# Splitting a token list's output in two, and placing the next one-hots later

## The chip, the cores and the metric

The kernel runs on one core of one Trainium2 chip. The metric is the device time of one execution in microseconds (us), of which the kernel before took 897.17 us (median of 3 runs, 896.05 to 897.62).

## What is computed

One decoder layer for 256 prompt tokens and 8 sample tokens of width 1024: a token mixer of four branches, then a mixture of experts with 64 SwiGLU experts of inner width 256, eight chosen for each token, and one shared expert, then a final norm. The change lies in the mixture of experts; of the reference that is

```python
def moe_ffn(h, router_w, router_bias, e_gate, e_up, e_down, s_gate, s_up, s_down):
    ...
    gates = jnp.zeros((n, N_EXPERTS), jnp.float32).at[jnp.arange(n)[:, None], idx].set(w)
    hg = jnp.einsum('nd,edf->nef', h, e_gate)
    hu = jnp.einsum('nd,edf->nef', h, e_up)
    act = jax.nn.silu(hg) * hu * gates[:, :, None].astype(h.dtype)
    routed = jnp.einsum('nef,efd->nd', act, e_down)
    shared = (jax.nn.silu(h @ s_gate) * (h @ s_up)) @ s_down
    return routed + shared
```

## The kernel before

**Jobs and groups.** The mixer and the routing take the first 356 us or so. After them the 64 experts are worked off as 64 jobs in 16 groups of four (i is the group, j the job). The experts are sorted by how many tokens they have. A job has room for 128, 64 or 32 rows: in a full group (3 to 13) the four jobs have 128, 32, 64 and 32 rows, in the light groups at the start and the end 32 or 64. Groups 4 to 12 run in a hardware loop of the same code. The rows of a group lie in two sheets of up to 128 rows: in a full group sheet 0 holds job 0, and sheet 1 jobs 1 to 3.

**Lists.** Which tokens belong to a job of the next group is found out during this group, one list in each job. VectorE writes one-hots (`one_hot`, L2167 to L2177, three instructions at L2176 that compare slot numbers with a row order), TensorE multiplies them by a table (`token_list`, L1188, products at L1199), and VectorE takes from the result the row numbers into `idx` (L2192 or L2195) and the gates into `gcol` (L2193 or L2196). Both stand in `list_out` (L2179), and only the second one counts up the semaphore `lst_ready`. TensorE's next list waits for it, as the bank is used again, and so does GpSimd, which starts the gather of a sheet (`gather`, L807 to L816) when all its lists are there. The gates of the next group take the place of those of this group, so `list_out` waits with `act_ready` for the gating of the same job of this group (L2188).

**A job on the engines.** TensorE: up products (`up`, L1231, products at L1246 for 32 rows, L1249 for 128, L1251 and L1252 for 64), in their middle the turning of the activations of the job before (L891), then the list products; in job 1 the sums of the sheets done so far (`sums`, L1312, eight sums of 264 columns in three banks, products at L1334); where a sheet is due, the turning of its gathered rows (`turn_rows`, L1203, products at L891); last the down products of the job before (L1283 for 32 rows, L1292 for 128, L1298 and L1301 for 64). ScalarE: silu (L1673), copy of half of the turned rows (L1657), activations (L1665), outputs (L1687, L1690). VectorE: gating, that is silu times up times gate (`gated`, L2224, L2232), the other half of the turned rows (`rows_out`, L2210, L2213), the additions of the sums (`add_sums`, L2281, L2289), the spreading of token numbers (`sheet_to_tokens`, L2274, L2278) and the low parts of the outputs (`y_out`, L2235, L2247). GpSimd has nothing but the gathers (L814) in this stage, each behind its lists and behind the turning of the sheet that had the buffer before.

**Order by hand.** Each engine has its own `body(i)`, and the order of the calls in it is the order on the engine. VectorE's is the one that changes (L2324). In job 0 of a full group it is gating, list of the next group, one-hots for the next list, copy of rows of sheet 1; in job 1 the additions stand there, in job 2 the spreading, and in job 3 the copy of rows of the next group's sheet 0; the outputs of the job before come last. TensorE's up products of job 1 wait for both copies of sheet 1. The fourth of the eight sums waits for the first addition, as it has the same bank, and the eighth for the sixth (L1327 and L1328).

**Weights.** SyncE loads the weights of each job, 3 x 1 MB: gate and up when the up products of the job four before have ended, down when its down products have (`reload`, L670, issues at L652, L653 and L656). There are four slots.

Of the kernel before, what the change touches and what calls it, by code (L numbers as in the profile page):

```python
# [11 lines left out]
ALU = mybir.AluOpType  # L12
# [49 lines left out]
LIST_BANK = 7  # L62
# [59 lines left out]
BIG = 4096.0  # L122
# [3 lines left out]
UNROLL = 4  # L126
# [3 lines left out]
FIXED = 2  # L130
# [26 lines left out]
def bass_decoder_step(nc, x_prompt, x_sample, state_conv, state_pool, state_conf, c_prompt, c_sample,  # L157
# [6 lines left out]
    with ExitStack() as ctx:  # L164
# [137 lines left out]
        def in_mid(n):  # L302
# [52 lines left out]
        names = """cnt_ready ld_c ya_ready v_stored row_out rows_spread sh_load ld_mod2 consts tables_zero x2_sq  # L355
                   sh_down_load h2_stored up_done down_done x_xt x_w tokens_in to_token_ready bank3_copied bank4_gated sum_full sum_taken token_taken acc_gated rest_zero last_sum x_fin x_gated x_added
                   fin_ready out_done pool_chain ld_stage wg_masked states_done w_hi w_lo h2_ready
                   lst_ready xt_done dma_may_go ys_act ys_dve x2_ready
                   ld_fin x_idx x_gat x_y x_sc st_stored c_silu
                   x_norm h_split v_ready ws_ready ld_param pooled_ready g2_rows dconv_ready sq_ready  # L360
                   y_split m_split sel_ready h_raw oh_ready list_done act_ready
# [94 lines left out]
        def rows_used(i, j):  # L456

            if isinstance(i, int) and i == 0:
                return ROWS_OF_FIRST_JOB[j]
            return (ROWS_OF_END_JOB if end_group(i) else ROWS_OF_LIGHT_JOB if light_group(i) else ROWS_OF_JOB)[j]  # L460
# [13 lines left out]
        def first_group(i):  # L474

            return isinstance(i, int) and i == 0
# [62 lines left out]
        def slots_of(i, j):  # L539

            return max(rows_used(i, j), HALF)
# [173 lines left out]
        def _(pool):  # L715
# [91 lines left out]
            def gather(i, s):  # L807

                lists = UNROLL * i + max(j for j in range(UNROLL) if place_of(i, j)[0] == s) + 1
                at = buffer_of(i, s)  # L810
                need(pool, S["xt_done"], sheet_of(i, s) - 1)
                pool.wait_ge(S["lst_ready"], lists)
                pool.sem_inc(S["dma_may_go"], 1)
                g.indirect_dma_start(out=xg[at], out_offset=None, in_=h_table,  # L814
                                     in_offset=bass.IndirectOffsetOnAxis(ap=idx[:, s, 0:1].bitcast(mybir.dt.uint32), axis=0),
                                     bounds_check=last_token, oob_is_err=False).then_inc(gathered[at], 16)  # L816
# [943 lines left out]
        def _(ve):  # L1760
# [8 lines left out]
            def link(ins):  # L1769

                ve.wait_ge(S["dve_chain"], mark(ins))
# [404 lines left out]
                    last = V.tensor_scalar(hot[:, j % 2, t, 0:n], order[:], p, None, ALU.is_equal)  # L2176
                last.then_inc(S["oh_ready"], 1)  # L2177

            def list_out(i, j):  # L2179

                e = UNROLL * i + j
                ve.wait_ge(S["list_done"], e + 1)
                n, m = slots_of(i, j), rows_used(i, j)
                b = psum[0:n, LIST_BANK, :]
                place = idx[rows_at(i, j), place_of(i, j)[0], :]
                if not first_group(i):
                    ve.wait_ge(S["token_taken"], i)
                    ve.wait_ge(S["act_ready"], e - 3)  # L2188
                    if j == 1 and light_group(i - 1) and not light_group(i):
                        ve.wait_ge(gathered[buffer_of(i - 1, 1)], 16 * (i + 1))  # L2190
                if first_group(i) and j < FIXED:
                    V.tensor_scalar(place, b[0:m, 0:1], BIG, None, ALU.add)  # L2192
                    V.tensor_copy(gcol[0:n, j, :], b[:, 1:2]).then_inc(S["lst_ready"], 1)  # L2193
                else:
                    V.tensor_scalar(place, b[0:m, 0:1], b[0:m, 1:2], BIG, ALU.add, ALU.add)  # L2195
                    V.tensor_scalar(gcol[0:n, j, :], b[:, 2:3], b[:, 3:4], b[:, 4:5], ALU.add, ALU.add).then_inc(S["lst_ready"], 1)  # L2196

            def rows_unused(s):

                return V.tensor_scalar(idx[HALF + QUARTER:CAP, s, :], zeros[HALF + QUARTER:CAP, 0:1], BIG, None, ALU.add)  # L2200
# [9 lines left out]
            def rows_out(i, s):  # L2210
                ve.wait_ge(S["xt_done"], sheet_of(i, s) + 1)
                need(ve, S["up_done"], jobs_before_buffer(i, s))
                V.tensor_copy(xgT[buffer_of(i, s)][:, 4:8, :], psum[:, 6, :].rearrange("p (k c) -> p k c", k=4)).then_inc(S["xgt_dve"], 1)  # L2213
# [10 lines left out]
            def gated(i, j):  # L2224

                e = UNROLL * i + j
                ve.wait_ge(S["silu_ready"], e + 1)
                need(ve, S["tact_done"], e - 1)
                n = slots_of(i, j)
                width = P if rows_used(i, j) == QUARTER else FE  # L2230
                b = psum[:, j % 2, FE:2 * FE] if n == CAP else psum[0:n, j % 2, 0:width]
                V.scalar_tensor_tensor(act[0:n, j % 2, 0:width], b, gcol[0:n, j, :], silu[0:n, j % 2, 0:width],  # L2232
                                       ALU.mult, ALU.mult).then_inc(S["act_ready"], 1)
# [90 lines left out]
            def body(i, first=False, last=False):  # L2324
                before_last = isinstance(i, int) and i == LAST - 1
                for j in range(UNROLL):
                    prev = not (first and j == 0)
                    pi, pj = (i if j else i - 1), (j - 1) % UNROLL
                    if j == 0:
                        take_tokens(i)  # L2330
                    if light_group(i + 1) and not light_group(i) and j == 0:
                        ve.wait_ge(S["token_taken"], i + 1)
                        link(rows_unused(0))
                        if first:
                            link(rows_unused(1))
                    gated(i, j)
                    if not last:
                        list_out(i + 1, j)
                    if not last and j < UNROLL - 1:
                        one_hot(i + 1, j + 1)  # L2340
                    elif not last and not before_last:
                        one_hot(i + 2, 0)
                    if end_group(i + 1) and not end_group(i) and j == 1:
                        link(rows_unused(1))
                    if first and j == 1:
                        ve.wait_ge(S["tokens_in"], 1)
                        link(V.tensor_copy(token_order, token_order.bitcast(I32)))
                        for s in range(2):
                            sheet_to_tokens(i, s)
                    if sums_at(i, j):  # L2350
                        add_sums(i)
                    if first and j == UNROLL - 1:
                        sheet_to_tokens(i, 2)
                    if not first and j == 2:
                        for s in range(2):
                            sheet_to_tokens(i, s, rounded=not last)
                    if next_sheet(i, j):
                        rows_out(*next_sheet(i, j))
                    if last and j:
                        gated_out(pj)  # L2360
                    elif prev:
                        y_out(pi, pj)
                    if last and j == 1:
                        gate_sums()
                    if first and j == UNROLL - 1:
                        rows_beyond()
# [138 lines left out]
```

## Time and profile before

| | |
|---|---|
| Median of 3 runs | 897.17 us |
| The profiled execution | 896.34 us |
| Its span | 894.0 us |
| TensorE busy | 846.1 us (95%) |
| VectorE busy | 565.9 us (63%) |
| ScalarE busy | 308.9 us (35%) |
| GpSimd busy | 50.5 us (6%) |
| DMA, mean over the span | 331 GB/s |

The profile is of one execution. A busy share is an average over the stages; in the second half TensorE is busy in nine tenths or more of each slice of the span, and so are the 16 DMA engines. In the rows, a bracket behind an instruction is the idle time of its engine ahead of it and what the profile holds for the releaser; PE is TensorE, PEld its weight loads, DVE VectorE, ACT ScalarE, POOL GpSimd, SPq the queue of SyncE. "DMA to landing" is the time from an issue to the arrival of the whole transfer.

### The profile page before, as it was taken

To read this page: it belongs to the slowest core of one execution; us is meant where nothing else is said; L and a number is where in the kernel's file an instruction comes from. 1 tells how busy PE (TensorE), PEld (TensorE's weight loads), DVE (VectorE), ACT (ScalarE), POOL (GpSimd) and SP (SyncE) were. 2 spreads that over 40 slices of the span, in tenths; PEclk is the share of its full clock that TensorE was granted. 3 is DMA by queue.
4 is the path that set the end of the run, shared out by engine and by line. 5 is a ranking of instruction groups with operands and counts; after the bars stand their busy time and mean duration, and the time that the engine had idled before them with its cause. 6 is when DMAs were issued, how large, how long until landed. Compare 5 with 4: busy or idle time off the path is not lost.

```text
span 894.0 us, 21073 instructions
## 1 busy us (share of the span) xinstructions
PE 846.1 (95%) x7872; PEld 639.8 (72%) x7872; DVE 565.9 (63%) x1425; ACT 308.9 (35%) x588; POOL 50.5 (6%) x92
## 2 busy tenths in 40 slices
PE   4799999999999998999999999999999999999995
PEld 2599999999999997657665556656556555666662
DVE  2458888899996878537554555546546455555555
ACT  3564444344428513022322322223232232223323
POOL 2010000000000000100000000000000000000000
PEclk9899999999999999899999999999999999999999
DMA  9984556888976746899999999999999999999961
GB/s 338 344 261 157 174 170 227 274 310 272 320 261 236 242 140 261 336 372 409 396 419 411 389 415 413 418 407 414 424 414 411 422 414 409 416 418 403 419 251 49
DMA packets 92711, 295.93 MB, mean 331 GB/s; under 512 B 7718, under 2 KB 45670, under 8 KB 67659
## 3 DMA queue, kind: packets, MB, share of 16 engines
q1 hardware_dynamic: 86139, 280.55, 81.8%
q0 software_dynamic: 6016, 13.10, 3.9%
q10 hardware_dynamic: 489, 1.33, 0.4%
q8 instruction: 48, 0.79, 0.3%
q14 instruction: 19, 0.16, 0.0%
HBM read 300.19 MB, written 4.14 MB: 340 GB/s over the span
## 4 chain that ended last, share of the span: by engine, by line
PE 68%; DVE 17%; DMA 7%; issue 6%; ACT 1%; SPq 0%; DVEq 0%; POOLq 0%; ACTq 0%
PE psum L887 19%; PE psum L1251 8%; PE psum L891 7%; DMA xn<-h_table,idx 6%; PE psum L1249 6%; PE psum L1246 6%; PE psum L1334 5%; PE psum L1292 5%; DVE mid L1927 4%; DVE wexp_r L1800 4%; PE psum L1298 3%; PE psum L1283 3%; DMA wexp<-in_ada_w 2%; PE psum L1331 1%; PE psum L1145 1%
## 5 line engine op out<-in xcount | busy, mean ns | idle before, releaser
L887 PE MATMUL psum<-xn_r,wexp_r 128*128 128x264 f32 x1024 | 193.8, 289 | 5.9 <-DVE hT_r L1838 5.9
L887 PEld LDWEIGHTS psum<-xn_r,wexp_r 128*128 128x128 f32 x1024 | 161.7, 191 | 8.2 <-issue 7.8
L887 PE MATMUL psum<-hT_r,wexp_r 128*128 128x264 f32 x512 | 146.3, 286 | 0.0
L1800 DVE TENSOR_TENSOR wexp_r<-wexp,wexp_r 128x1024 fp32r<-128x1024 f32 x88 | 106.5, 1217 | 20.7 <-ACT wexp_r L1510 20.3
L1510 ACT ACTIVATE wexp_r<-wexp 128x1024 fp32r<-128x1024 f32 x88 | 92.3, 1054 | 57.2 <-PE psum L887 44.5
L2232 DVE SCALAR_TENSOR_TENSOR hT<-psum,gcol,hT 64x256 f32<-64x256 f32 (+2 forms) x64 | 26.4, 413 | 133.8 <-ACT hT L1673 133.1
L887 PEld LDWEIGHTS psum<-hT_r,wexp_r 128*128 128x128 f32 x512 | 97.8, 191 | 0.1
L1249 PE MATMUL psum<-wexp,mid 128*128 128x512 f32 x208 | 94.7, 599 | 1.7 <-issue 0.9
L2247 DVE TENSOR_TENSOR bc_r<-psum,xn_r 32x256 fp32r<-32x256 f32 (+2 forms) x136 | 65.9, 485 | 27.0 <-ACT xn_r L1690 15.1
L1252 PE MATMUL psum<-wexp,mid 128*64 128x256 f32 x320 | 77.3, 384 | 0.0
L1251 PE MATMUL psum<-wexp,mid 128*64 128x256 f32 x320 | 77.2, 384 | 0.0
L1249 PEld LDWEIGHTS psum<-wexp,mid 128*128 128x128 f32 x208 | 37.4, 190 | 50.2 <-issue 50.0
L1246 PE MATMUL psum<-wexp,mid 128*32 128x128 f32 x1984 | 69.2, 278 | 3.6 <-issue 3.6
L887 PE MATMUL psum<-wexp_r 128*128 128x264 f32 (+1 forms) x512 | 71.4, 284 | 0.0
L887 PEld LDWEIGHTS psum<-wexp_r 128*128 128x128 f32 x512 | 66.8, 188 | 0.9 <-issue 0.9
L1246 PEld LDWEIGHTS psum<-wexp,mid 128*32 128x32 f32 x1984 | 54.3, 108 | 16.9 <-ACT mid L1657 9.0
L1251 PEld LDWEIGHTS psum<-wexp,mid 128*64 128x64 f32 x320 | 41.1, 136 | 32.7 <-issue 13.7
L814 POOL DMA_INDIRECT xn<-h_table,idx x33 | 33.1, 1002 | 460.5 <-DVE gcol L2196 340.2
L1334 PE MATMUL psum<-hT_r,mT_r 128*128 128x264 f32 x240 | 54.1, 307 | 5.0 <-DVE mid L2289 4.0
L2289 DVE TENSOR_TENSOR mid<-mid,psum 128x264 f32<-128x264 f32 x120 | 48.9, 425 | 13.8 <-PE psum L1334 11.4
L1673 ACT ACTIVATE hT<-psum 64x256 f32<-64x256 f32 (+2 forms) x64 | 21.1, 330 | 91.8 <-PE psum L1249 41.4
L2247 DVE TENSOR_TENSOR mT_r<-psum,mT_r 128x512 fp32r<-128x512 f32 (+2 forms) x42 | 25.8, 614 | 40.0 <-ACT mT_r L1690 37.4
(343 smaller groups left out, 1332.1 us busy)
## 6 DMA issues: line engine op xcount, KB each, us to landing
wexp<-in_e_gate SPq DMA_DIRECT2D x64, 1024.0 KB, 9.5
wexp<-in_e_up SPq DMA_DIRECT2D x64, 1024.0 KB, 11.7
wexp<-in_e_down SPq DMA_DIRECT2D x64, 1024.0 KB, 10.7
wexp<-in_w_in SPq DMA_DIRECT2D x32, 1024.0 KB, 5.9
mid<-in_ada_w SPq DMA_DIRECT2D x8, 2048.0 KB, 9.9
wexp<-in_w_branch SPq DMA_DIRECT2D x8, 1024.0 KB, 5.3
wexp<-in_ada_w SPq DMA_DIRECT2D x14, 512.0 KB, 10.8
wexp<-in_w_out SPq DMA_DIRECT2D x4, 1024.0 KB, 5.8
```

Source lines behind the costliest of these rows:

```text
L887: last = mm(out, a[x], b[y], start=start and x == y == 0, stop=stop and x == 1)
L891: return nc.tensor.transpose(out, src, ident[0:rows, 0:rows])
L1246: last = mm(psum[q * QUARTER:(q + 1) * QUARTER, j % 2, 0:P], x[:, k, :], w[:, k, 1 - q // 2, q % 2:FE:2], start=(k == 0), stop=(k == KT - ...
L1249: last = mm(psum[:, j % 2, :].rearrange("p (a f) -> p a f", a=2), x[:, k, :], w[:, k], start=(k == 0), stop=(k == KT - 1))
L1251: mm(psum[HALF:CAP, j % 2, 0:FE], x[:, k, :], w[:, k, 0], start=(k == 0), stop=(k == KT - 1), tile_position=(0, HALF))
L1252: last = mm(psum[0:HALF, j % 2, 0:FE], x[:, k, :], w[:, k, 1], start=(k == 0), stop=(k == KT - 1), tile_position=(0, 0))
L1292: last = mm(psum[:, 3 + h, :], a[:, f, :], w[:, f, h * BLK:(h + 1) * BLK], start=(f == 0), stop=(f == 1))
L1334: last = mm(out, as_r(y[:, c * P:(c + 1) * P]), as_r(to_token[:, a, :]), start=((b, a) == sheets[0] and y is y_sheets[b][0] and not shared ...
L1510: F(as_r(high(u, q)), low(u, q), ACT.Copy).then_inc(S["w_hi"], 1)
L1800: V.tensor_tensor(as_r(low(u, q)), low(u, q), as_r(high(u, q)).bitcast(F32), ALU.subtract).then_inc(S["w_lo"], 1)
L2247: last = V.tensor_tensor(as_r(low[rows, a]), whole, as_r(high[rows, a]).bitcast(F32), ALU.subtract)
L2289: V.tensor_tensor(accT[:, c, :], accT[:, c, :], out, ALU.add).then_inc(S["sum_taken"], 1)
```

## The change

`list_out` is split into `list_rows` (the row numbers, with a new semaphore `idx_ready`) and `list_gates` (the gates, with `lst_ready` as before). GpSimd's gather waits for `idx_ready`. In VectorE's body `list_rows(i + 1, j)` is called ahead of `gated(i, j)` and `list_gates(i + 1, j)` behind it. The call of `one_hot` moves from there to behind the additions, the spreading and the copy of rows, ahead of the outputs. `list_out` remains, as both in a row, for the first group. The wait for the gathered rows at the change from light to full groups goes with the row numbers.

```diff
-                pool.wait_ge(S["lst_ready"], lists)
+                pool.wait_ge(S["idx_ready"], lists)
...
-            def list_out(i, j):
+            def list_rows(i, j):
 
                 e = UNROLL * i + j
                 ve.wait_ge(S["list_done"], e + 1)
-                n, m = slots_of(i, j), rows_used(i, j)
-                b = psum[0:n, LIST_BANK, :]
+                b = psum[0:rows_used(i, j), LIST_BANK, :]
                 place = idx[rows_at(i, j), place_of(i, j)[0], :]
                 if not first_group(i):
                     ve.wait_ge(S["token_taken"], i)
-                    ve.wait_ge(S["act_ready"], e - 3)
                     if j == 1 and light_group(i - 1) and not light_group(i):
                         ve.wait_ge(gathered[buffer_of(i - 1, 1)], 16 * (i + 1))
                 if first_group(i) and j < FIXED:
-                    V.tensor_scalar(place, b[0:m, 0:1], BIG, None, ALU.add)
+                    V.tensor_scalar(place, b[:, 0:1], BIG, None, ALU.add).then_inc(S["idx_ready"], 1)
+                else:
+                    V.tensor_scalar(place, b[:, 0:1], b[:, 1:2], BIG, ALU.add, ALU.add).then_inc(S["idx_ready"], 1)
+
+            def list_gates(i, j):
+
+                n = slots_of(i, j)
+                b = psum[0:n, LIST_BANK, :]
+                if not first_group(i):
+                    ve.wait_ge(S["act_ready"], UNROLL * i + j - 3)
+                if first_group(i) and j < FIXED:
                     V.tensor_copy(gcol[0:n, j, :], b[:, 1:2]).then_inc(S["lst_ready"], 1)
                 else:
-                    V.tensor_scalar(place, b[0:m, 0:1], b[0:m, 1:2], BIG, ALU.add, ALU.add)
                     V.tensor_scalar(gcol[0:n, j, :], b[:, 2:3], b[:, 3:4], b[:, 4:5], ALU.add, ALU.add).then_inc(S["lst_ready"], 1)
+
+            def list_out(i, j):
+
+                list_rows(i, j)
+                list_gates(i, j)
...
+                    if not last:
+                        list_rows(i + 1, j)
                     gated(i, j)
                     if not last:
-                        list_out(i + 1, j)
-                    if not last and j < UNROLL - 1:
-                        one_hot(i + 1, j + 1)
-                    elif not last and not before_last:
-                        one_hot(i + 2, 0)
+                        list_gates(i + 1, j)
...
                     if next_sheet(i, j):
                         rows_out(*next_sheet(i, j))
+                    if not last and j < UNROLL - 1:
+                        one_hot(i + 1, j + 1)
+                    elif not last and not before_last:
+                        one_hot(i + 2, 0)
                     if last and j:
                         gated_out(pj)
```

## Rows read from the trace of the kernel before

**Rows 1.** VectorE's timeline of one group: start us, us, line, operation, tiles [idle before].

```profile
603.01 0.48 DVE L2232 SCALAR_TENSOR_TENSOR hT<-psum,gcol,hT 128x256 f32<-128x256 f32 x1 [5.84 <-ACT hT L1673]
...
603.87 0.57 DVE L2176 TENSOR_SCALAR mod_room<-row_order_quarter,cmp_ 128x64 bf16<-128x64 f32 x3
604.35 0.69 DVE L2213 COPY mid<-psum 128x512 f32<-128x512 f32 x1
...
608.15 0.34 DVE L2232 SCALAR_TENSOR_TENSOR hT<-psum,gcol,hT 64x128 f32<-64x128 f32 x1 [0.86 <-ACT hT L1673]
...
608.96 0.56 DVE L2176 TENSOR_SCALAR mod_room<-row_order_half,cmp_ 128x64 bf16<-128x64 f32 x3
609.44 1.09 DVE L2289 TENSOR_TENSOR mid<-mid,psum 128x264 f32<-128x264 f32 x3
...
634.95 0.48 DVE L2232 SCALAR_TENSOR_TENSOR hT<-psum,gcol,hT 128x256 f32<-128x256 f32 x1 [5.83 <-ACT hT L1673]
```

**Rows 2.** TensorE's timeline of the same group.

```profile
603.64 1.07 PE L1283 MATMUL psum<-wexp,hT 128*32 128x256 f32 x16
605.13 1.15 PE L1246 MATMUL psum<-wexp,mid 128*32 128x128 f32 x32 [0.42 <-issue]
...
607.71 0.26 PE L1199 MATMUL psum<-router,mod_room 128*64 x3
...
609.91 0.51 PE L1334 MATMUL psum<-hT_r,mT_r 128*128 128x264 f32 x2 [0.29 <-DVE mid L2289]
```

**Rows 3.** ScalarE's timeline, its half of the turned rows.

```profile
603.75 0.60 ACT L1657 ACTIVATE mid<-psum 128x512 f32<-128x512 f32 x1 [0.86 <-PE psum L891]
```

**Rows 4.** The waits from 466 to 819 us: total us, times, longest us.

```profile
PEld psum L1334 <- DVE mid L2289: 8.9, 22, 0.9
...
PE psum L891 <- DMA xn<-h_table,idx: 3.1, 5, 0.8
PE psum L1246 <- issue: 2.9, 7, 0.6
```

**Rows 5.** Stretches: us, busy us (x instructions) by engine, PEclk, DMA share, GB/s.

```profile
411.00:860.00 449.00, 434.69 (x4222) 274.46 (x4223) 241.69 (x710) 128.88 (x315) 29.70 (x29) 1.00 1.01 413
...
600.00:616.00 16.00, 15.13 (x142) 10.04 (x140) 8.85 (x26) 3.74 (x9) 1.00 (x1) 1.00 1.02 424
...
424.00:428.00 4.00, 3.87 (x88) 2.69 (x87) 2.38 (x5) 2.63 (x7) 0.00 (x0) 1.00 0.80 279
...
588.00:592.00 4.00, 4.00 (x93) 2.93 (x88) 3.00 (x11) 2.21 (x7) 0.00 (x0) 1.00 0.93 358
```

**Rows 6.** The last up weights' issue and landing; TensorE's start on them.

```profile
L653 SPq DMA_DIRECT2D wexp<-in_e_up x1: 1255/1255/1255, 842.1 to 842.1; - x1
...
DMA to landing us min/median/max: 18.1/18.1/18.1
...
864.15 1.10 PE L1246 MATMUL psum<-wexp,mid 128*32 128x128 f32 x32
```

**Rows 7.** Gather behind job 3: VectorE, GpSimd, the chain's turning; 19 gathers' landings.

```profile
624.58 0.34 DVE L2232 SCALAR_TENSOR_TENSOR hT<-psum,gcol,hT 64x128 f32<-64x128 f32 x1
...
625.29 0.28 DVE L2196 TENSOR_SCALAR gcol<-psum 64x1 f32<-64x1 f32 x1
...
626.36 1.00 POOL L814 DMA_INDIRECT xn<-h_table,idx  x1 [20.62 <-DVE gcol L2196]
...
634.49 1.16 PE psum L891 x8
...
DMA to landing us min/median/max: 7.8/8.4/9.8
```

**Rows 8.** The page: the gathers' queue; the issues of gate weights.

```profile
q0 software_dynamic: 6016, 13.10, 3.9%
...
wexp<-in_e_gate SPq DMA_DIRECT2D x64, 1024.0 KB, 9.5
```

**Rows 9.** Gathers from 820 to 845 us.

```profile
DMA to landing us min/median/max: 7.7/8.0/8.2
```

More of the change, by code:

```diff
@@ L357, in bass_decoder_step @@
                    fin_ready out_done pool_chain ld_stage wg_masked states_done w_hi w_lo h2_ready
-                   lst_ready xt_done dma_may_go ys_act ys_dve x2_ready
+                   lst_ready idx_ready xt_done dma_may_go ys_act ys_dve x2_ready
                    ld_fin x_idx x_gat x_y x_sc st_stored c_silu
```

## The prediction

> **What bounds the kernel now.** I read the page first, then the timeline of one repeating group of four experts on each engine, then the waits, and last the DMA queue, because two resources look full. The groups of four repeat every 31.94 us (gating of job 0 at 603.01 and at 634.95) [rows 1]. In such a group TensorE has two holes where it waits for VectorE. The first stands in front of the up products of job 1: the down products before it end at 604.71, the next product starts at 605.13 [rows 2]. Those products need both halves of the turned rows; ScalarE's half is copied by 604.35 [rows 3], VectorE's half only from 604.35 to 605.04, as VectorE first does the gating, the row numbers, the gates and three one-hots [rows 1]. So the profile's releaser (ScalarE, or "issue") is not the last one; VectorE is. The second hole is inside the sums: the fourth sum starts at 609.91 after 0.29 us of idle [rows 2], because its bank is freed by the first addition, which starts at 609.44, right behind the one-hots of 608.96 [rows 1]. A third wait comes and goes: the turning of gathered rows waits for the gather itself.
>
> From 466 to 819 us, which holds the eleven full groups, the waits view adds these up: 2.9 us before up products, 3.1 us for gathers, and 8.9 us of weight loads held by the additions in 22 places, two to a group [rows 4]. The second place of a group (the eighth sum waits for the sixth addition) does not depend on what stands ahead of the additions and stays; the first is the larger one, and I take 0.45 us a group for it, between its visible 0.29 us of idle and what the loads show in both places together (8.9/11 = 0.81).
>
> The second resource is DMA. Over 411 to 860 us its share is 1.01 at 413 GB/s [rows 5]. TensorE nevertheless never waits for an expert's weights there, since they land early. But the lead shrinks at the end: the last up weights are issued at 842.1 and need 18.1 us, so they land at 860.2, and TensorE starts on them at 864.15 [rows 6]. That is a lead of 3.95 us, and it is the number that limits this change.
>
> **The change, part by part.** *Row numbers ahead of the gating.* The same instruction, about 0.2 us, moves ahead of the gating, into a stretch in which VectorE waits for silu. For job 0 it costs nothing, as VectorE is idle before 603.01. It adds a wait: the gating is now behind the list products. For job 1 these end at 607.97 [rows 2], and the gating used to start at 608.15 [rows 1], so with 0.2 us of work in between the gating starts about 0.1 us late. Who waits for it is the turning of the activations, which comes half an up product later; for job 1 that is behind all the sums. I cost it at nothing; without that cover it would be 0.1 us in two jobs of a group, 3 us in all.
>
> *Own semaphore.* GpSimd no longer waits for the gates. The gather behind job 3 is released at present by the gates, which end at 625.57, and starts on GpSimd at 626.36, 0.79 us later [rows 7]. In the new order the row numbers are written as soon as the preceding work of VectorE ends, about 624.6 (the gating of job 3 at 624.58 began there without idle time [rows 7]), so the gather starts at about 625.4, some 0.95 us earlier against TensorE. Its landing takes 7.8 to 9.8 us, median 8.4 [rows 7]: 633.8 by the median. TensorE turns those rows at 634.49 when nothing holds it [rows 7]. So the waits of 3.1 us for gathers go, all but the rare 9.8 us one. GpSimd's queue holds only these gathers, and the one for the large list, released by job 0, merely starts earlier; its rows are not turned before job 3. No DMA is added.
>
> *One-hots behind copies and sums.* Three instructions, in the row of job 0 from 603.87 to 604.44 [rows 1], move behind the copy of rows, behind the additions, or behind the spreading of token numbers. The copy can then start at 603.8 (gating to 603.49, gates of 0.28 us as in [rows 7]), beside the down products, and end at 604.5, before they end at 604.71. The 2.9 us go. The additions start at about 608.9, so the first hole in the sums goes: 11 x 0.45 = 5.0 us. What is late next: the list products need these one-hots. For job 1 the one-hots end about 605.1 and the products come at 607.7 [rows 2]; the tightest place is job 2, where one-hots, spreading and list products follow each other within 3 us and about 1 us is left. The copies of outputs behind them wait for ScalarE anyway.
>
> Sum for TensorE: 2.9 + 3.1 + 5.0 = **11.0 us** in the full groups. Light groups have the same holes and I leave them out of the sum, as room for holes that stay.
>
> *Can DMA follow?* A group loads twelve transfers of 1.049 MB and two gathers of 13.10/33 = 0.40 MB [rows 8], 13.4 MB. At the 424 GB/s of a stretch with a deep queue [rows 5] that is 31.6 us, only 0.35 us under the present period, while TensorE alone would want 30.9. So the queue becomes deeper, group by group. In the middle nothing is felt: the leads are far longer there. At the end TensorE meets the last up weights. They can land earlier only by what DMA idles now. **Bounds:** from below, the shares of eight stretches of 4 us in which the queue runs low (0.80 in the deepest, 0.93 in a typical one [rows 5]) lack some 0.8 + 7 x 0.33 = 3.1 us. From above, moving the same bytes at 424 instead of 413 GB/s would save 449 x 11/424 = 11.6 us. A transfer is only done when its slowest engine is, so its loss is larger than the mean share says, but short dips also come from the gathers' and instruction packets, which stay. I take **4.5 us**, near the lower bound, since the share is what counts idleness directly.
>
> The last up weights then land at 855.7, and the start on them moves from 864.15 to there: 3.95 + 4.5 = **8.45 us**, less than TensorE's 11. What follows them (last down products, last sums, final norm) isn't touched. The profiled execution took 896.34 us around a span of 894.0; it gives 887.9. The median of the runs shown is 897.17, 0.83 higher, so the time is **888.7 us**.
>
> By the Trainium skill, "DMA: Bandwidth & Descriptors", section "Where 436 GB/s comes from", the ceiling of the ports is 435 GB/s; an estimate from it is 30.8 us a group, and DMA would then let TensorE have its 11 us. The trace shows 424 with a deep queue, and no stretch of 16 us at the page's value; I go by the trace.
>
> **The rivals.** *TensorE gets all its holes back.* If DMA has more in it than the deep stretches show, the limit is TensorE: 11.0 us, with the light groups' holes some 12: 885.7. For it: TensorE waits for no weights now. Against it: share 1.01. *The DMA stream cannot end earlier.* If the dips stay, only the lead of 3.95 us is won: 893.2. For it: a dip can be packets of other queues. Against it: the share falls in the dips, so engines stand idle there, which packets of other queues would not do. *Little changes.* If VectorE's gating behind the list products and the holes that stay eat the gain, or a hole is ended by ScalarE after all, the time is within 1.8 us: 896. Against it: ScalarE's copy had ended 0.78 us before.
>
> *Slower: the gather.* A deeper queue could make each gather slower. Its place is the turning of rows in job 0; released at 625.4, it makes TensorE wait from a landing time of 9.0 us on. With the gathers' part gone the gain is 2.9 + 5.0 = 7.9 us, or 0.72 a group, so the kernel is slower from about 9.7 us on. At 10.3 us, half a microsecond over the longest, each full group loses 1.3: 14.3 - 7.9 = 6.4 us slower, 903.6. Against it: between 820 and 845 us, where the weights' landings are the longest, the gathers took 7.7 to 8.2 us [rows 9]. By the Trainium skill, same page, "Queues, rings and completion order", an engine takes turns between queues, so a gather isn't behind another queue's backlog; the trace agrees so far.
>
> **How the numbers follow.** Forecast 0.58 (own range 885.7 to 891.7, from the unknown 4.5 us taken between 1.5 and 7.5); all holes back 0.15; stream fixed 0.15; little 0.06; slower 0.06. What a measurement of this kernel can tell from no change is about 0.2%, 1.8 us. Faster by more: 0.58 + 0.15 + 0.15 = 0.88; same 0.06; slower 0.06. The range reaches from the full gain, a little beyond, to the fixed stream: 884.5 to 893.7; left outside are the last two cases and the tails.
>
> **What would show it.** In the changed kernel's timeline: row numbers just ahead of the gating, VectorE's copy of rows starting with ScalarE's, no idle before the up products of job 1, and none before the fourth sum. Full groups of 30.9 to 31.6 us. Landings of weights that lengthen from group to group, and in the last group a TensorE wait for weights of the last one or two experts. It is wrong if TensorE waits for weights nowhere and the gain is over 10 us (DMA had more in it), if the holes stay, or if the turning waits for gathers longer than 3.1 us in sum.

## The result, and the profile after

The kernel with the change takes **889.67 us** (median of 6 runs, 889.15 to 891.01) against 897.00 us for the kernel before in the same session (6 runs, 895.44 to 897.62). The ratio is 0.9923, with an interval of 0.9911 to 0.9936: 7.3 us faster. The forecast was 888.7 with a range of 884.5 to 893.7. The profiled execution took 889.15 us around a span of 886.8, 7.2 us less than before by both numbers.

The page of the kernel after: its chain of work that ended last, two groups of up products, and the issues of gate weights.

```profile
PE 70%; DVE 15%; DMA 11%; issue 2%; ACT 1%; SPq 0%; DVEq 0%; POOLq 0%; ACTq 0%
...
L1251 PE MATMUL psum<-wexp,mid 128*64 128x256 f32 x320 | 78.7, 389 | 2.3 <-DMA wexp<-in_e_up 2.3
...
L1246 PE MATMUL psum<-wexp,mid 128*32 128x128 f32 x1984 | 70.2, 280 | 5.0 <-DMA wexp<-in_e_up 4.5
...
wexp<-in_e_gate SPq DMA_DIRECT2D x64, 1024.0 KB, 13.3
```

In the chain that ended last DMA has 11% of the span, 7% before, and "issue" 2%, 6% before. Up products now wait for up weights, 4.5 + 2.3 = 6.8 us in all. In the kernel before they never did. A gate transfer takes 13.3 us from issue to landing (the median of 64), 9.5 before [rows 8]: the queue is deeper.

**VectorE** in one full group of the kernel after (compare [rows 1]):

```profile
595.12 0.22 DVE L2192 TENSOR_SCALAR idx<-psum 128x1 int32<-128x1 f32 x1 [5.13 <-PE psum L1199]
595.64 0.48 DVE L2244 SCALAR_TENSOR_TENSOR hT<-psum,gcol,hT 128x256 f32<-128x256 f32 x1 [0.30 <-ACT hT L1673]
596.16 0.29 DVE L2203 TENSOR_SCALAR gcol<-psum 128x1 f32<-128x1 f32 x1
596.37 0.68 DVE L2225 COPY mid<-psum 128x512 f32<-128x512 f32 x1
596.97 0.57 DVE L2176 TENSOR_SCALAR mod_room<-row_order_quarter,cmp_ 128x64 bf16<-128x64 f32 x3
...
600.82 3.20 DVE L2301 TENSOR_TENSOR mid<-mid,psum 128x264 f32<-128x264 f32 x7
604.38 0.43 DVE L2301 TENSOR_TENSOR mid<-mid,psum 128x264 f32<-128x264 f32 x1 [0.36 <-PE psum L1334]
```

The row numbers stand in a hole ahead of the gating, and the gating still waits 0.30 us for ScalarE: in job 0 the step costs nothing. The copy of rows follows the gates, the one-hots follow the copy and, in job 1, all eight additions (they start at 604.73). The first seven additions run without a gap; only the eighth still waits for TensorE.

**TensorE** in the same group and at the start of the next (compare [rows 2]):

```profile
594.86 0.22 PE L1199 MATMUL psum<-router,mod_room 128*128 x3
594.94 1.14 PE L891 MATMUL psum<-ident,xn 128*128 128x128 f32 x8
596.00 1.07 PE L1283 MATMUL psum<-wexp,hT 128*32 128x256 f32 x16
597.15 1.14 PE L1246 MATMUL psum<-wexp,mid 128*32 128x128 f32 x32
...
599.70 0.26 PE L1199 MATMUL psum<-router,mod_room 128*64 x3
...
603.59 0.51 PE L1334 MATMUL psum<-hT_r,mT_r 128*128 128x264 f32 x2
...
611.79 1.07 PE L1283 MATMUL psum<-wexp,hT 128*32 128x256 f32 x16
612.67 1.09 PE L1246 MATMUL psum<-wexp,mid 128*32 128x128 f32 x32
...
617.80 0.59 PE L1301 MATMUL psum<-wexp,hT 128*64 128x512 f32 x1
618.32 0.70 PE L1249 MATMUL psum<-wexp,mid 128*128 128x512 f32 x1
```

and five more rows of TensorE in the kernel before, at the same places:

```profile
602.23 0.22 PE L1199 MATMUL psum<-router,mod_room 128*128 x3
602.56 1.15 PE L891 MATMUL psum<-ident,xn 128*128 128x128 f32 x8
...
612.17 0.52 PE L1334 MATMUL psum<-hT_r,mT_r 128*128 128x264 f32 x2
...
626.39 0.59 PE L1301 MATMUL psum<-wexp,hT 128*64 128x512 f32 x1
627.09 0.69 PE L1249 MATMUL psum<-wexp,mid 128*128 128x512 f32 x1
```

Read as distances from start to start, before and after: list products to the turning of gathered rows 0.33 and 0.08; down products (L1283) to the up products of job 1, 1.49 [rows 2] and 1.15; list products of job 1 to the eighth sum 4.46 and 3.89; last down products to the up products of the next group 0.70 and 0.52. The savings are 0.25, 0.34, 0.57 and 0.18, together 1.34 us. The up products of job 1 come again at 627.70, 30.55 us after 597.15; the period before was 31.94 [rows 1], so 1.39 us less.

**The waits** of the kernel after from 460 to 810 us (compare [rows 4]):

```profile
PEld psum L1246 <- ACT mid L1657: 4.4, 10, 0.5
...
PEld psum L1334 <- DVE mid L2301: 2.7, 11, 0.3
...
PE psum L891 <- DMA xn<-h_table,idx: 0.2, 1, 0.2
```

The gathers cost 0.2 us instead of 3.1, the additions hold weight loads in 11 places instead of 22, and the profile shows no idle time of TensorE before the up products of job 1. It still names ScalarE's copy as the releaser of weight loads there, though VectorE's copy (596.37 + 0.68 = 597.05) is the later one. The place is not quite free: from the start of the down products to that of the up products it is 1.15 us in job 1, and 0.88 in job 3 (611.79 to 612.67), where no copy of rows is awaited. So of some 0.6 us a group 0.34 went and 0.27 is left, behind VectorE's copy. No gap stands before the fourth sum either: the next one in the sums is the small one at 603.59, where the eighth sum waits for the sixth addition.

**What is late next.** TensorE's starts on the weights of three of the last experts in the kernel after, and on the very last one (a fourth wait, of 0.28 us, is at 802.09):

```profile
810.22 0.76 PE L1246 MATMUL psum<-wexp,mid 128*32 128x128 f32 x17 [2.97 <-DMA wexp<-in_e_up]
...
834.15 0.40 PE L1251 MATMUL psum<-wexp,mid 128*64 128x256 f32 x1 [2.06 <-DMA wexp<-in_e_up]
...
842.30 0.67 PE L1246 MATMUL psum<-wexp,mid 128*32 128x128 f32 x16 [1.48 <-DMA wexp<-in_e_up]
...
857.13 0.73 PE L1246 MATMUL psum<-wexp,mid 128*32 128x128 f32 x17
```

and the issue of the last up weights in the kernel after:

```profile
L653 SPq DMA_DIRECT2D wexp<-in_e_up x1: 1823/1823/1823, 829.6 to 829.6; - x1
...
DMA to landing us min/median/max: 27.3/27.3/27.3
```

They land at 829.6 + 27.3 = 856.9, and TensorE starts on them 0.25 us later, at 857.13. Before they landed at 860.2 and the start was at 864.15 [rows 6]. The start came forward by 7.0 us, of which 3.3 is the stream's and 3.7 the lead that was used up. Of the 7.2 us 7.0 are there. What TensorE had gained beyond this it lost again: it began group 13 at 770.96 us instead of 786.44, 15.5 us ahead, as the next two rows show (after, then before):

```profile
770.96 0.70 PE L1249 MATMUL psum<-wexp,mid 128*128 128x512 f32 x1
```

```profile
786.44 0.70 PE L1249 MATMUL psum<-wexp,mid 128*128 128x512 f32 x1
```

Not all of what it lost is idle time. From the start of group 13 to the start on the last up weights the kernel after takes 86.2 us; e4 (below), where TensorE waits for no weights, takes 75.8 (770.87 to 846.71). Of these 10.3 us 6.8 are the waits above, and 0.3 is the last landing: the last up products start 1.20 us after the down products ahead of them (855.93), and 0.88 would do. The other 3.2 or so are a lower clock. In the first row TensorE's granted clock (the third number from the end) is 0.50, the lower of its two levels (1.2 and 2.4 GHz), behind the wait of 2.97 us; the second row is e1 (below), behind a wait of 3.08 us:

```profile
811.40:814.40 3.00, 3.00 (x38) 2.15 (x39) 0.21 (x1) 0.55 (x2) 0.00 (x0) 0.50 0.99 412
```

```profile
842.50:848.50 6.00, 5.95 (x73) 4.76 (x74) 0.65 (x2) 0.55 (x2) 0.00 (x0) 0.50 1.00 415
```

From 836 to 838 us, behind the wait of 2.06 us, it was 0.50 again, and from 842 to 857, behind the one of 1.48, it was 1.00. In the kernel after this costs nothing in the end, since TensorE meets a later landing all the same. In e1, e6 and e7 the long wait comes so late that it does cost time.

The stretch of full groups in the kernel after (columns as in [rows 5]):

```profile
411.00:850.00 439.00, 430.25 (x4203) 273.85 (x4203) 244.90 (x707) 127.62 (x313) 28.74 (x29) 0.99 1.01 419
600.00:616.00 16.00, 15.96 (x166) 11.10 (x167) 9.79 (x29) 3.97 (x11) 0.00 (x0) 1.00 1.02 422
```

The DMA share was 1.01 before and is 1.01 now; over the whole stretch only the rate tells that the queue ran low now and then, 413 GB/s before [rows 5] and 419 now.

### The profile page after: what moved, and what is told of

It reads as the page before. It is cut to its first block, busy times and chain, and to the rows that moved or that the text cites. A ratio compares the mean times of both kernels' runs of the same rounds, so it can differ in the third digit from the quotient of the medians.

```text
span 886.8 us, 21071 instructions
## 1 busy us (share of the span) xinstructions
PE 844.9 (95%) x7872; PEld 640.5 (72%) x7872; DVE 570.6 (64%) x1425; ACT 309.0 (35%) x588; POOL 50.9 (6%) x92
## 4 chain that ended last, share of the span: by engine, by line
PE 70%; DVE 15%; DMA 11%; issue 2%; ACT 1%; SPq 0%; DVEq 0%; POOLq 0%; ACTq 0%
PE psum L887 18%; PE psum L1249 9%; PE psum L1334 7%; PE psum L1251 6%; DMA wexp<-in_e_up 6%; PE psum L891 6%; PE psum L1246 5%; PE psum L1292 5%; DVE wexp_r L1800 4%; DVE mid L1927 4%; PE psum L1298 3%; PE psum L1283 3%; DMA xn<-h_table,idx 2%; DMA wexp<-in_ada_w 2%; DMA wexp<-in_w_in 1%
## 5 line engine op out<-in xcount | busy, mean ns | idle before, releaser
L2192 DVE TENSOR_SCALAR idx<-psum 32x1 int32<-32x1 f32 (+2 forms) x62 | 13.4, 216 | 117.5 <-PE psum L1199 116.5
L1251 PE MATMUL psum<-wexp,mid 128*64 128x256 f32 x320 | 78.7, 389 | 2.3 <-DMA wexp<-in_e_up 2.3
L1252 PE MATMUL psum<-wexp,mid 128*64 128x256 f32 x320 | 78.8, 390 | 0.0
L2301 DVE TENSOR_TENSOR mid<-mid,psum 128x264 f32<-128x264 f32 x120 | 50.7, 428 | 13.8 <-PE psum L1334 10.0
L1927 DVE SCALAR_TENSOR_TENSOR mid<-wexp,prm,mid 128x256 f32<-128x256 f32 x120 | 49.7, 473 | 0.0
## 6 DMA issues: line engine op xcount, KB each, us to landing
wexp<-in_e_gate SPq DMA_DIRECT2D x64, 1024.0 KB, 13.3
```

Source lines behind the costliest of these rows:

```text
L1251: mm(psum[HALF:CAP, j % 2, 0:FE], x[:, k, :], w[:, k, 0], start=(k == 0), stop=(k == KT - 1), tile_position=(0, HALF))
L1252: last = mm(psum[0:HALF, j % 2, 0:FE], x[:, k, :], w[:, k, 1], start=(k == 0), stop=(k == KT - 1), tile_position=(0, 0))
L1927: taps[c] = mark(V.scalar_tensor_tensor(dcv[:, c, 0:SEQ], gluP[:, c, h:h + SEQ], w, dcv[:, c, 0:SEQ], ALU.mult, ALU.add))
L2301: V.tensor_tensor(accT[:, c, :], accT[:, c, :], out, ALU.add).then_inc(S["sum_taken"], 1)
```

## The experiments

Twelve kernels ran, each in five rounds beside the kernel before, whose medians in the three sessions were 896.55 (17 runs), 896.62 (15) and 897.05 (9). Ratios are against the kernel before in the same session. The theory was: TensorE's holes go in full, and the weight stream gives back only 8 us or so of them. The rivals were that the holes are worth no more than what was seen, and that one of the three parts does it all.

| kernel | median us | ratio (interval) |
|---|---|---|
| the change | 889.67 | 0.9923 (0.9911 to 0.9936) |
| e4: the change, down loads cut | 879.71 | 0.9810 (0.9798 to 0.9823) |
| e5: before, down loads cut | 896.51 | 0.9996 (0.9988 to 1.0005) |
| e6: the change, down loads cut by 1/32 | 886.72 | 0.9885 (0.9870 to 0.9900) |
| e1: one-hots moved only | 892.16 | 0.9956 (0.9940 to 0.9972) |
| e9: e1, down loads cut | 887.79 | 0.9893 (0.9877 to 0.9908) |
| e2: row numbers and semaphore only | 890.55 | 0.9926 (0.9912 to 0.9939) |
| e10: e2, down loads cut | 890.12 | 0.9923 (0.9909 to 0.9937) |
| e3: semaphore only | 896.63 | 0.9999 (0.9990 to 1.0009) |
| e7: one-hots of job 1 ahead of the sums | 889.02 | 0.9914 (0.9900 to 0.9928) |
| e8: gather released by the gates | 889.14 | 0.9918 (0.9904 to 0.9932) |
| e11: e8, down loads cut | 883.19 | 0.9853 (0.9839 to 0.9866) |
| e12: shared expert's work in group 3 | 890.39 | 0.9926 (0.9913 to 0.9940) |

### Is it the weight stream?

**e4** and **e5** load three quarters of each expert's down weights; e4 in the kernel after, e5 in the kernel before. The edit of both:

```diff
-                sp.dma_start(wexp[:, s, 4096:6144], rows_of_expert(down_v, e)).then_inc(down_full[s], 16)
+                sp.dma_start(wexp[:, s, 4096:5632], rows_of_expert(down_v, e)[:, 0:1536]).then_inc(down_full[s], 16)
```

and the second half of the down products reads from 512 columns earlier, so that their number and sizes stay. **e6** does the same in the kernel after with 64 columns instead of 512, so that 31/32 are loaded.

> The changed kernel with only three quarters of each job's down weights loaded; the down products of the second half read an overlapping part, so their results differ while instructions and sizes stay. That takes 64 x 0.26 = 16.8 MB, some 40 us, out of the weight stream. Theory (stream caps the gain): the waits for weights in the last groups, 6.9 us in all, vanish and the time falls to 882 to 883.5 us. Rival (TensorE itself limits the changed kernel): 889 to 890, as before the cut.

> The kernel before with the same cut of its down loads (the second half of the down products reads an overlapping part). Theory: that kernel has no wait for weights, so it stays within its gather waits: 894 to 897 us, and the change is worth 12 to 14 us between this kernel and the changed one with the cut, against 7.3 with all weights. Rival (DMA holds the kernel before too): it falls by several us, to 890 or less.

> The changed kernel with 31/32 of each job's down weights loaded (second half of the down products overlapping by 64 columns): 64 x 32 KB = 2.1 MB less, about 5.0 us of the stream. Theory: the last weights land 5 us earlier, TensorE waits some 2 us instead of 6.9, 884.5 to 885.5 us. Rival (TensorE limits): no change, 889 to 890.

The kernel before gained nothing from a quarter less down weights: 896.51 us, ratio 0.9996. The kernel after fell to 879.71. So the same change is worth 16.8 us (896.51 to 879.71; I had expected 12 to 14) where the stream has room and 7.3 where it hasn't. The waits of e4 from 466 to 819 us hold no weights at all:

```profile
PEld psum L1338 <- DVE mid L2305: 3.0, 12, 0.3
PE psum L895 <- DMA xn<-h_table,idx: 1.5, 4, 0.5
```

(lines are shifted by 4 there). Its stretch of full groups (411 to 840 us) moves 396 GB/s, less than the queue can. In e5 the share is 0.95 at 382 GB/s (411 to 850 us).

e4 was faster than I expected by 2 to 4 us. I had taken 6.9 us of waits off the 889.7 of the kernel after; 3.1 us more went, about as much as the lower clock behind those waits (3.2, above). e6 leaves out 64 x 1.049 MB / 32 = 2.1 MB, which is 5 us at 419 GB/s, and gained 3.0 us over the kernel after (889.67 to 886.72; 3.7 in the profiled executions). It missed its range by 1.2 us, and up products still waited 4.2 + 1.9 us for weights where I expected 2. The trace shows the stream's part whole and the rest lost on TensorE: the last up weights landed at 825.3 + 26.9 = 852.2, 4.7 us earlier than in the kernel after, but TensorE started on them only at 853.57, 3.6 us earlier. It waited for nothing there. It had waited for the weights of the job two before the last,

```profile
837.73 1.93 PE L1250 MATMUL psum<-wexp,mid 128*32 128x128 f32 x32 [2.98 <-DMA wexp<-in_e_up]
```

and its clock was 0.50 from 837.7 to 840.7 us. From this start to the one on the last up weights it took 15.8 us, in e4 14.9 (831.85 to 846.71).

### Which part brings what?

**e1** is the kernel before with the one-hots in their new place only:

```diff
-                    if not last and j < UNROLL - 1:
-                        one_hot(i + 1, j + 1)
-                    elif not last and not before_last:
-                        one_hot(i + 2, 0)
...
                     if next_sheet(i, j):
                         rows_out(*next_sheet(i, j))
+                    if not last and j < UNROLL - 1:
+                        one_hot(i + 1, j + 1)
+                    elif not last and not before_last:
+                        one_hot(i + 2, 0)
```

**e2** is the kernel after with that block back behind `list_gates(i + 1, j)`. **e3** is the kernel before with the semaphore alone: the two writes of row numbers count up `idx_ready`, and the gather waits for it.

```diff
-                pool.wait_ge(S["lst_ready"], lists)
+                pool.wait_ge(S["idx_ready"], lists)
...
-                    V.tensor_scalar(place, b[0:m, 0:1], b[0:m, 1:2], BIG, ALU.add, ALU.add)
+                    V.tensor_scalar(place, b[0:m, 0:1], b[0:m, 1:2], BIG, ALU.add, ALU.add).then_inc(S["idx_ready"], 1)
```

> The kernel before with the one-hots moved behind the copies of rows, the additions and the spreading, and nothing else. Theory (VectorE's one-hots make TensorE's holes, and the weight stream caps what closing them brings at about 7 us): the copy of rows and the additions start early, a full group takes about 30.8 us, TensorE gets to the last group over 10 us early and waits for weights there; 889.5 to 891.5 us. Rival A (the gathers, released by a semaphore of their own, bring the gain): 894 us or more. Rival B (no cap, each part brings its own share): 897.0 minus 8 to 9 and later additions from the other part.

> The changed kernel with the one-hots put back to where they were, ahead of the copies and the additions: row numbers ahead of the gating and the semaphore of their own alone. Theory: the waits for gathers (3.1 us) go, and the copy and the additions start some 0.2 us earlier as one instruction less is ahead of them; a full group takes 31.3 to 31.5 us; 5 to 6 us less for TensorE, little wait for weights: 890.5 to 893 us. Rival A (own semaphore brings the gain): 889.5 to 890.5. Rival C (only the one-hots count): 896 to 897.

> The kernel before with the gathers released by the row numbers through a semaphore of their own, the order on VectorE unchanged. The gather starts only 0.3 us earlier (the gates' time). Theory: part of the 3.1 us of gather waits goes, 895 to 896.5 us. Rival A: 892 or less.

e2 came out as expected. e3 lies 0.1 us above its range: the waits for gathers shrink as expected, and the time does not. e1 lies 0.7 us above its range. Its waits from 466 to 819 us:

```profile
PE psum L891 <- DMA xn<-h_table,idx: 6.1, 10, 1.2
PEld psum L1334 <- DVE mid L2289: 3.0, 12, 0.3
...
PEld psum L891 <- DMA xn<-h_table,idx: 1.7, 3, 1.2
```

The additions hold 3.0 us instead of 8.9 [rows 4], as in the kernel after, but the gathers are now waited for 7.8 us instead of 3.1. The gather is released by VectorE late in job 3 and TensorE comes to its rows sooner, so the hole moves there. But this is not what sets e1's time: it began group 13 at 776.88, 9.6 us ahead of the kernel before, more than the stream lets through. Its last up weights landed at 857.1, as in the kernel after, and TensorE started on them at 859.71, 2.6 us later. These are its last wait for weights and that start:

```profile
842.55 1.93 PE L1246 MATMUL psum<-wexp,mid 128*32 128x128 f32 x32 [3.08 <-DMA wexp<-in_e_up]
...
859.71 1.10 PE L1246 MATMUL psum<-wexp,mid 128*32 128x128 f32 x32
```

Between them lie 17.2 us, against 14.8 in the kernel after (842.30 to 857.13). The 2.3 us more go with the clock, at 0.50 from 842.5 to 848.5 us (the 32 products of the first row take 1.93 us, 1.14 in the kernel after), and no later wait takes them up. Without them e1 would have been in its range, at some 889.9 (an estimate from the two distances).

e3 shows the reverse trade, over the same stretch:

```profile
PE psum L1246 <- issue: 5.1, 9, 0.7
...
PE psum L891 <- DMA xn<-h_table,idx: 1.6, 4, 0.8
```

The wait for gathers halves, from 3.1 to 1.6 us, and the idle time before the up products of job 1 grows from 2.9 to 5.1. Those products end one chain behind the turning: rows turned earlier only wait for VectorE's copy, which has not moved. Hence 896.63 us, no change.

### The parts with room in the stream

**e9**, **e10** and **e11** are e1, e2 and e8 (below) with the cut of e4. I ran them because the stream's cap hides what a part brings.

> The kernel before with only the one-hots moved, and three quarters of the down weights loaded (second half of the down products overlapping), so that the stream of weights caps nothing. Theory: TensorE's own gain shows; in the uncut run TensorE reached group 13 at 776.9 us against 786.4 before, so 10 to 11 us against the cut kernel before (896.5): 885.5 to 887 us. If one-hots and row numbers add up, this part and the next one give 16.8 us together.

> Row numbers ahead of the gating with their own semaphore, one-hots in the old place, with the same cut stream. Theory: TensorE reached group 13 at 780.5 us against 786.4 in the uncut run, so 6 to 7 us: 889.5 to 890.5 us, hardly less than with the full stream (890.55), as this part alone is just about what the stream allows. Rival (this part is worth as much as the whole change): 885 or less.

> The changed kernel with the gathers released by the gates again, with the same cut stream. Theory: the earlier release of gathers is worth what the cap hid, about 4 us by the time at which group 13 began (775.0 against 771.0 us): 882.5 to 885 us against 879.7. Rival (the semaphore is worth nothing): 880.

e10 and e11 came within their ranges, e9 0.8 us above. It began group 13 at 779.65, 2.8 us later than e1, with more waits for gathers, here from 466 to 819 us:

```profile
PE psum L895 <- DMA xn<-h_table,idx: 7.7, 10, 1.6
...
PEld psum L895 <- DMA xn<-h_table,idx: 1.6, 2, 1.2
```

With room in the stream the one-hots bring 897.05 - 887.79 = 9.3 us, row numbers with the semaphore 897.05 - 890.12 = 6.9, both 16.8: the parts add up within the spread (16.2). With the full stream they bring 4.4 and 6.1, and both 7.3 rather than 10.5. The full stream takes 4.9 us from the one-hots alone and 0.9 from the other part. Not all of the 4.9 is the cap: from the start of group 13 to the start on the last up weights e1 takes 82.8 us and e9 76.5, and of these 6.3 us 3.9 are waits for weights and the rest, 2.4, is the clock. e11 against e4 gives the worth of the semaphore in the finished order: 883.19 against 879.71, 3.5 us, with gathers waited for 7.1 us in e11 and 2.0 in e4.

### The finished order with one step undone

**e7** puts the one-hots of job 1 back ahead of the sums; **e8** lets the gather wait for the gates again.

```diff
+                        if j == 1:
+                            one_hot(i + 1, j + 1)
...
-                    if not last and j < UNROLL - 1:
+                    if not last and j < UNROLL - 1 and j != 1:
                         one_hot(i + 1, j + 1)
-                    elif not last and not before_last:
+                    elif not last and j == UNROLL - 1 and not before_last:
```

```diff
-                pool.wait_ge(S["idx_ready"], lists)
+                pool.wait_ge(S["lst_ready"], lists)
```

> The changed kernel with the one-hots of job 1 back ahead of the additions; those of jobs 0, 2 and 3 stay late. Theory: the hole in the sums comes back, 0.4 us a full group or 4.6 us to TensorE up to the last group, but TensorE waits for weights 6.9 us there, so it is hidden: 889.5 to 890.5 us, with waits for weights of only 2 to 3 us. Rival (TensorE limits): 894.

> The changed kernel with the gathers waiting for the gates again; order on VectorE as changed. Theory: gathers start 0.6 us later, TensorE's turning waits up to 0.3 us a group, hidden by the cap: 889.5 to 890.5 us. Rival A: 893 or more.

Both took what the kernel after takes (889.02 and 889.14, 0.5 and 0.4 us below their ranges), though each has its hole back, e7 in part. The waits of e7 from 466 to 819 us, and behind them, in a fence of their own, those of e8:

```profile
PEld psum L1334 <- DVE mid L2301: 7.4, 24, 0.5
```

```profile
PE psum L891 <- DMA xn<-h_table,idx: 3.6, 7, 1.2
```

Against the kernel after over the same stretch that is 4.5 us more of weight loads held in e7 and, with 1.0 us of weight loads that waited for gathers, 4.4 us more of gathers in e8, and the medians show nothing of it. The waits for weights at the end shrink in their place, from 6.8 us to 4.7 in e7 (expected were 2 to 3) and 5.6 in e8; one profile of each does not balance to the microsecond. e8 against e11 is the clearest case: the same step undone is invisible with the full stream and costs 3.5 us without it.

### A try to get more

If the stream is the limit, it should start earlier. **e12** is the kernel after with the work of the shared expert's first layer in group 3 instead of groups 1 and 2, so that the light groups pass sooner and loads are issued sooner.

```diff
-SHARED_IN = {1: (0,), 2: (1,)}
+SHARED_IN = {3: (0, 1)}
```

> The changed kernel, complete, with the shared expert's part of the sums taken in group 3 instead of groups 1 and 2. In groups 1 and 2 the stream of weights idles now and then, as TensorE frees slots late; 2 us less work for TensorE there bring the loads forward. Theory (only idle time of the stream before it is full for good can still be won): 0.5 to 1.5 us less than the changed kernel, 888 to 889 us, though TensorE has the same work. Rival (TensorE limits): no difference, 889.7.

It missed: 890.39 us, no better than the kernel after. The loads did come forward (the up weights of the first job of group 3 landed at 450.9 instead of 452.5), but TensorE was then busy in group 3 with the moved work while the queue ran low. From 464 to 495 us the rate was 390 GB/s, and 418 in the kernel after. The stretch from 488 to 492 us, in e12 and then in the kernel after:

```profile
488.00:492.00 4.00, 4.00 (x54) 2.48 (x54) 1.06 (x5) 0.67 (x3) 0.00 (x0) 1.00 0.94 320
```

```profile
488.00:492.00 4.00, 4.00 (x78) 2.86 (x77) 2.39 (x9) 1.87 (x5) 0.00 (x0) 1.00 1.01 410
```

By these rates the 31 us lose some 2 us of stream (an estimate), no less than was won: the last up weights of e12 landed at 856.9 again. No complete kernel I ran beats the one with the change by more than the spread.

## Why the prediction was right

The time was 1.0 us over the forecast, and the mechanism is the forecast one: TensorE's holes go, and DMA hands back only a part. Step by step:

- **Which engine ended the holes.** Right. The profile named ScalarE or "issue" before the up products of job 1; moving VectorE's one-hots took the idle time away while ScalarE's copy stayed where it was (1.2 us behind the start of the turning in both kernels). The distances between starts show 0.27 us a group left.
- **Row numbers ahead of the gating, at nothing.** Right in job 0, where the gating still waits for ScalarE. For job 1 the step showed at no place of TensorE.
- **The gathers' 3.1 us.** Right: 0.2 us is left. The lead was worked out too large: the gather starts 8.6 us ahead of the turning (616.87 to 625.48) and not 9.1 (625.4 to 634.49), in part since the instruction that writes the row numbers takes 0.2 us itself, which the working left out. And e3 shows that the semaphore alone would have brought nothing: in the old order its hole passes on to the up products of job 1. In the finished order it is worth 3.5 us (e11 against e4).
- **The sum of 11.0 us for TensorE.** Too low: 15.5 by group 13, and 16.8 with room in the stream. A full group took 30.55 us, below the 30.9 to 31.6 forecast. TensorE was 1.8 us ahead at the start of group 3 (464.28 instead of 466.10), and ten groups at 1.37 us make the rest of the 15.5. Against my 1.0 us a group the sums bring 0.12 more (0.57 instead of 0.45), the copy in job 1 0.08 more (0.34 instead of 2.9/11), the gathers 0.03 less, and 0.18 comes from a place I left out: in job 3 one-hots stood ahead of the copy of rows for the next group as well. The 1.8 us lie ahead of group 3, in groups that I left out.
- **The cap.** Right in kind, and e4 with e5 shows it as a cause. Of its two terms the lead of 3.95 us came out as 3.7, since TensorE started 0.25 us after the landing. The idle time of the stream that could be won was the mis-sized one: 3.3 us instead of the 4.5 taken. It is nearly the 3.1 of the lower bound, so the shares of the short stretches were the thing to go by, without the surcharge. With 3.7 + 3.3 = 7.0 the forecast would have been 890.2. That the cap alone sets the time is partly luck: the forecast has no term for the clock behind a long wait. In the kernel after these waits come early enough to be absorbed, in e1 a late one costs 2.3 us.
- **Where TensorE meets the weights.** Half right. Of the 6.8 us of waits 3.3 fall in group 14, and only 3.5 in the last group, where I had put them all. As TensorE's gain was 4 to 5 us larger than I thought, it caught up with the stream earlier.
- **The ceiling of the ports.** By the Trainium skill, "DMA: Bandwidth & Descriptors", section "Where 436 GB/s comes from", 435 GB/s is the ceiling, and by the estimate from it (30.8 us a group) TensorE would have kept the 11 us forecast. The runs decide for the trace: with a deep queue the rate was 422 GB/s over 16 us and 419 over 439 us.
- **The rivals.** All holes back (885.7; 11.0 and 12 us under the median give 886.2 and 885.2) needs fewer bytes than this kernel loads, as in e4; a fixed stream (893.2) fell, as its end moved by 3.3 us; the time did fall, and the gathers did not become slower (below).

## What to carry to other kernels

Before a hole on the busiest engine is priced, look at the lead of its prefetches at the *end* of the stage (first use minus landing): here the holes were worth that lead plus what the stream still idled, 3.7 + 3.3 us, and undoing a step in the finished kernel then shows nothing of its worth. To see what a part brings, run it once with some bytes cut from the stream: if the kernel before does not change under the cut, the cut is clean. Look at the granted clock behind each long wait of TensorE: the wait can cost more than its own length, and near the end nothing absorbs the rest. And waits that follow one another at one place (a gather, then a copy) are best taken away together; e3's alone handed its time to the next.

## What the runs showed of the hardware that I had not expected

**Gathers beside a deep queue.** Up weights issued in the stretch from 660 to 760 us took twice as long to land in the kernel after as in the kernel before (after, then before):

```profile
DMA to landing us min/median/max: 16.9/22.0/25.8
```

```profile
DMA to landing us min/median/max: 7.1/11.2/13.7
```

The 14 gathers of the kernel after between 616.9 and 815.1 us took what the gathers took before [rows 7]:

```profile
DMA to landing us min/median/max: 7.9/8.2/9.7
```

Twice the depth of SyncE's queue did not show in them. By the Trainium skill, "DMA: Bandwidth & Descriptors", section "Queues, rings and completion order", an engine takes turns between the queues it has work for; the trace agrees with that.

**The stream's end is stiff.** In the kernel after and in e12 the last up weights landed at 856.9, in e7 at 829.5 + 27.2 = 856.7 and in e1 at 831.1 + 26.0 = 857.1, although the loads of e12 began earlier and e1 and e7 keep holes of TensorE that the kernel after has not. In e2, whose queue is less deep there, they landed at 835.4 + 23.5 = 858.9; for e8 the profile holds no landing of them. From the kernel before to the kernel after the issue moved by 12.5 us (842.1 to 829.6) and the landing by 3.3. Only the kernel after and e12 start on them right behind this landing; e1 and e7 come 2.6 and 1.1 us later, because of the clock.

**A long wait slows TensorE behind it.** Behind single waits of 2.98 to 3.08 us for weights the granted clock was 0.50 for 3 us in e6 and e7 and for 6 us in e1. The same work from there to the last up weights took 15.8 us in e6, 15.9 in e7 and 17.2 in e1, and 14.8 in the kernel after and 14.9 in e4.

**A full DMA share costs nothing by itself.** The kernel before, at a share of 1.01, lost nothing to DMA: with a quarter of the down weights, a twelfth of an expert, cut away it took the same time at a share of 0.95 (e5).
